# A hybrid decoder step: the state-space stage rebuilt in token layout, its projections split into three rounded products, and 16 dense steps placed beside the decode rows

## The reference, cut to what matters

```python
xbc, ssm_buf_new = causal_dwconv(xbc, ssm_buf, ssm_conv_w)
xbc = jax.nn.silu(xbc + ssm_conv_b).astype(f32)
xs_, Bm, Cm = split_cols(xbc, (SSM_DINNER, SSM_BC, SSM_BC))
dt = jax.nn.softplus(dt_raw.astype(f32) + ssm_dt_bias.astype(f32))
y_b, ssm_S_new = ssd_chunked(xs_, dt, A, Bm, Cm, ssm_S)      # per chunk:
#   y = (C B^T * decay) (x dt) + decay_in * (C S);  S = S * decay + B^T (decay_out * x dt)
y_b = (y_b + ssm_D[:, None] * xs_) * silu(z)
y_b = rmsnorm(y_b over each of 8 groups of 256 columns, ssm_norm_w)
```

## Time and profile before

| | |
|---|---|
| median of 3 runs | 3957.24 us (3954.14 to 3958.15) |
| profiled execution | 3952.51 us, span 3950.8 us |
| mean granted TensorE clock | 0.939 of full speed |
| TensorE matmuls busy | 3638.9 us (92%) |
| TensorE weight loads busy | 3120.4 us (79%) |
| VectorE | 1690.2 us (43%) |
| ScalarE | 843.3 us (21%) |
| GpSimd | 852.6 us (22%) |
| chain that ended last | TensorE 74%, VectorE 9%, issue 8%, ScalarE 3% |

### The profile page before, as it was taken

One profiled execution on the slowest core, in us unless ns is written; L12 is line 12 of the kernel. 1 busy time (PEld: TensorE's weight loads), 2 busy tenths in 40 slices (PEclk: granted clock), 3 DMA queues, 4 the chain that ended last, 5 costly groups with the idle time before them and its releaser, 6 DMA issues.

```text
span 3950.8 us, 53368 instructions
## 1 busy us (share of the span) xinstructions
PE 3638.9 (92%) x20671; PEld 3120.4 (79%) x20671; DVE 1690.2 (43%) x2840; ACT 843.3 (21%) x1709; POOL 852.6 (22%) x389
## 2 busy tenths in 40 slices
PE   6899999998899999999999977999988899999998
PEld 5888898887899766666666655667975799999998
DVE  4655556556300246566656671112024333323143
ACT  4333233333211122122212220001123111101010
POOL 3222323222122000000000000000322444444452
PEclk8999999998899999999999978999987899999999
DMA  3111011111222222212221225112422111111111
GB/s 113 45 44 39 28 32 38 43 38 33 71 81 70 63 65 77 79 52 59 76 81 49 76 88 198 59 43 64 134 69 85 32 53 44 43 48 48 47 44 64
DMA packets 317893, 248.31 MB, mean 63 GB/s; under 512 B 11028, under 2 KB 293213, under 8 KB 317717
## 3 DMA queue, kind: packets, MB, share of 16 engines
q1 hardware_dynamic: 282798, 211.28, 17.6%
q10 hardware_dynamic: 34992, 35.58, 2.6%
HBM read 200.50 MB, written 46.78 MB: 63 GB/s over the span
## 4 chain that ended last, share of the span: by engine, by line
PE 74%; DVE 9%; issue 8%; ACT 3%; POOL 2%; DMA 2%; ACTq 0%; DVEq 0%; SPq 0%; POOLq 0%
PE psum L894 22%; PE psum L1292 8%; PE psum L1294 8%; PE psum L1293 8%; PE psum L912 3%; PE psum L913 3%; PE psum L914 3%; PE psum L1028 2%; PE psum L1036 2%; PE psum L1040 2%; PE psum L868 2%; POOL wle L2687 1%; PE psum L1260 1%; PE psum L1323 1%; PE psum L1186 1%
## 5 line engine op out<-in xcount | busy, mean ns | idle before, releaser
L894 PE MATMUL psum<-xn,slab 128*128 128x344 f32 x2688 | 824.0, 464 | 29.4 <-ACT arena L1682 17.8
L894 PEld LDWEIGHTS psum<-xn,slab 128*128 128x128 f32 x2688 | 513.5, 194 | 304.3 <-issue 37.9
L2766 POOL TENSOR_SCALAR wparts<-slab 128x1024 fp32r<-128x1024 f32 x80 | 222.0, 2775 | 968.0 <-POOLq L68 968.0
L912 PE MATMUL psum<-xh,whe 128*128 128x344 f32 x1152 | 392.8, 341 | 16.3 <-POOL wle L2687 12.9
L913 PE MATMUL psum<-xl,whe 128*128 128x344 f32 x1152 | 373.2, 324 | 0.0
L914 PE MATMUL psum<-xh,wle 128*128 128x344 f32 x1152 | 372.4, 323 | 0.0
L1292 PE MATMUL psum<-at,wparts 128*128 128x344 f32 x960 | 308.8, 322 | 9.3 <-DVE r L2598 5.2
L1294 PE MATMUL psum<-at,wparts 128*128 128x344 f32 x960 | 307.6, 320 | 0.0
L1293 PE MATMUL psum<-xlow,wparts 128*128 128x344 f32 x960 | 306.9, 320 | 0.0
L2687 POOL TENSOR_TENSOR wle<-slab,whe 128x1024 fp32r<-128x1024 f32 x56 | 139.5, 2491 | 719.5 <-ACT whe L1433 719.5
L894 PE MATMUL psum<-arena,slab 128*128 128x344 f32 x768 | 229.1, 460 | 26.6 <-DMA arena<-d_yb 18.6
(11 more groups left out here) (385 smaller groups left out, 6319.7 us busy)
## 6 DMA issues: line engine op xcount, KB each, us to landing
slab<-in_w_in_dram SPq DMA_DIRECT2D x96, 512.0 KB, 4.0
arena<-d_rows SPq DMA_DIRECT2D x40, 512.0 KB, 5.1
slab<-in_w_ff_up_dram SPq DMA_DIRECT2D x32, 512.0 KB, 4.1
slab<-in_w_ff_down_dram SPq DMA_DIRECT2D x32, 512.0 KB, 3.9
out_dram<-arena ACTq DMA_DIRECT2D x24, 512.0 KB, 3.3
d_yb<-arena ACTq DMA_DIRECT2D x16, 516.0 KB, 5.9
...
```

The source lines that it names most:

```text
L894: mm = pe.matmul(psum[:, n, 0:GW], slabv[(base + u) % 2][:, k, :], src[:, k, n * GW:(n + 1) * GW], start=(k == 0 and u not in join), stop= ...
L912: pe.matmul(out, w_hi, a_hi, start=(k == 0), stop=False)
L2766: do(pool.tensor_scalar(rounded(wh[slot]), slab[slot][:, :], 1.0, None, ALU.mult))
```

## The change

- The projections of the state-space stage go through `project_parts`; slabs come in the order B, x, x, C, z, z; `high_weights` and `low_weights` are placed in ScalarE's and GpSimd's bodies; the sum of `xh` and `xl` is gone.
- The outputs are formed in token layout (`yt`): decay weights as stationary, x dt as moving operand; C times state is a product of its own, scaled on VectorE by `ecs`; z is transposed (tz) and multiplied in; the norm's sums come from ScalarE's squares with accumulation, the scale is applied on ScalarE, and 16 transposes (to0 to to3) turn y back.
- The decay differences move from VectorE to ScalarE (`decays`: eight relu with bias and one exp per tile). The broadcast decay rows come in four tiles of two chunks (`mlq`), the fourth over the first one once y1 is done.
- The skip term becomes a third product of the x transposes. The output tiles `yo` lie over `xdt` and `xdd`, so `wait(dve, yb_stored, 32 * g)` moves ahead of the x products.
- B and C of the sample rows are spread by products with a repeated column of the identity.
- `SFILL`: cb 24 becomes 8, decode 0 becomes 16.
- ScalarE's stores of the group before move behind the tb moves. In the last group SyncE issues the load of `ybv[0]` before the fourth decay tile.

Core of the diff:

```diff
+mlq = [carve(HPG * 2 * P) for _ in range(3)]
+mlq.append(mlq[0])
...
+yo = [arena[:, cut[0] - 4 * T + q * NT:cut[0] - 4 * T + (q + 1) * NT] for q in range(2)]
...
-SFILL = {"rw": 8, "tb": 8, "tx": 16, "cb": 24, "scan": 8, "fs": 8, "decode": 0, "norm": 16}
+SFILL = {"rw": 8, "tb": 8, "tx": 16, "cb": 8, "scan": 8, "fs": 8, "decode": 16, "norm": 16}
...
+    def csb_load(g, q):
+        last, group = ("y7", "y3", "y5", "y1")[q], g if q == 3 else g - 1
+        if not (isinstance(group, int) and group < 0):
+            sp.wait_ge(bank_full[ssm_plan.bank(last)], ssm_plan.after(last, group))
+            if not isinstance(group, int):
+                sp.sem_inc(sp_step, 1)
+        sp.dma_start(mlq[q].rearrange("p (r t) -> p r t", r=HPG),
+                     d_rows[bass.ds(HPG * g, HPG), q * 2 * P:(q + 1) * 2 * P].partition_broadcast(P)
+                     ).then_inc(csb_loaded[q % 3], 16)
...
+    def body(g, more, then):
         if more:
-            ssm_slab(g + 1, 0)
-            ssm_slab(g + 1, 1)
...
+            ssm_slab(g + 1, 3)
+        else:
+            upb_slab(0, 0, 0)
+            sp.wait_ge(yb_stored, 32 * SG_N // 2)
+            sp.wait_ge(proj_full, 3 * W_UPB)
+            sp.dma_start(ybv[0], d_yb[0:KT].rearrange("k p t -> p k t")).then_inc(yb_loaded[0], 16)
+        csb_load(g, 3)
+        if more:
+            ssm_slab(g + 1, 4)
+            csb_load(g + 1, 1)
+            csb_load(g + 1, 2)
+            ssm_slab(g + 1, 5)
+            csb_load(g + 1, 0)
+        if then:
+            ssm_slab(g + 2, 0)
+            ssm_slab(g + 2, 1)
...
+        project_parts(6 * g, W_SSM, m0, m1, lambda u, n: (proj_taken, 18 * g + (A_SSM + 3 * u + n - 2)),
+                      6 * [(xh, xl)])
...
+            def outputs(bk, c=c):
+                for r in range(HPG):
+                    head = slice(r * HD, (r + 1) * HD)
+                    yield pe.matmul(bk[:, head], cols(mlq[c // 2], 2 * r + c % 2),
+                                    xdt[:, 2 * P * c:2 * P * (c + 1)][:, head], start=True, stop=True)
                 if c:
...
+                    taken(G, f"su{c - 1}", g)
+                    yield pe.matmul(bk[:, 2 * P:4 * P], cols(cT, c), SST[c % 2], start=True, stop=True)
+
+            hand(G, f"y{c}", g, outputs)
+            if c == 1:
+                pe.wait_ge(z_ready, 2 * g + 2)
...
+                hand(G, f"tz{c // 2}", g, lambda bk, c=c: (
+                    pe.transpose(cols(bk, i), cols(zs[i % 2], c - 1 + i // 2), ident[:, :]) for i in range(4)))
             fill(f"scan{c}")
         taken(G, "su7", g)
...
+                hand(G, f"{name}{j}", g, lambda bk, j=j, part_=part_: (
+                    pe.matmul(cols(bk, i), ident[0:NB, 4 * j + i:4 * j + i + 1].broadcast_to([NB, P]),
+                              bc8[:, part_ * P:(part_ + 1) * P], start=True, stop=True) for i in range(4)))
...
+        pe.wait_ge(y8sq_ready, g + 1)
+        hand(G, "n8", g, lambda bk: (
+            pe.matmul(bk[:, 0:NB], ones[:, :], sq8[:, q * NB:(q + 1) * NB], start=(q == 0), stop=(q == 1))
+            for q in range(2)))
+        for p in range(4):
+            pe.wait_ge(ys_ready, NC * g + 2 * p + 2)
+            hand(G, f"to{p}", g, lambda bk, p=p: (
+                pe.transpose(cols(bk, i), yt[:, (2 * p + i % 2) * 2 * P + (i // 2) * P:][:, 0:P], ident[:, :])
+                for i in range(4)))
 
...
+    for u in range(6):
+        evacuate(0, 3 * u, 3 * u + 1)
+        high_weights((0, W_SSM + u + 1))
+        evacuate(0, 3 * u + 1, 3 * u + 3)
+        if 0 < u < 5:
+            stanh(0, u - 1)
...
+    def decays(g, q):
+
+        act.wait_ge(csb_loaded[q % 3], 16 * g + 16 if q in (1, 2) else 32 * g + 16 * (q // 3 + 1))
+        tile = mlq[q]
+        for i in range(2 * HPG):
+            r, c = i // 2, 2 * q + i % 2
+            ins = act.activation(cols(tile, i), cols(tile, i), ACT.Relu, scale=-1.0,
+                                 bias=shs[:, HPG * c + r:HPG * c + r + 1])
+        ins.then_inc(relu_ready, 1)
+        act.wait_ge(relu_ready, 4 * g + q + 1)
+        act.activation(tile, tile, ACT.Exp, scale=-1.0).then_inc(sdec_exp, 1)
...
-        for u in (4, 5):
...
         for j in range(2):
             move(G, f"tb{j}", g, half(btok, j), lambda bk: bk.rearrange("p (c i) -> p c i", c=4))
+        if not first:
+            stores(g - 1)
+        act.wait_ge(shs_ready, g + 1)
+        decays(g, 0)
         evac("tb")
...
+        if more:
+            high_weights((6 * g, W_SSM + 7))
+        act.activation(ecs, shs[:, 0:NC * HPG], ACT.Exp).then_inc(ecs_ready, 1)
+        decays(g, 1)
         evac("tx")
+        if more:
+            high_weights((6 * g, W_SSM + 8))
...
         evac("cb")
         for c in range(NC):
             evac(f"scan{c}")
             if more and c in (1, 3, 6):
-                stanh(g + 1, c // 2 if c < 6 else 2)
-        wait(act, stf_stored, 32 * g)
+                high_weights((6 * g, W_SSM + (9, 10, 11)[c // 2 - (c == 6)]))
+            if c == 2:
+                decays(g, 3)
+            if more and c in (2, 4, 6):
+                stanh(g + 1, c // 2 - 1)
+            if c >= 2:
+                squares(g, c - 2)
+        for c in range(NC - 2, NC):
+            squares(g, c)
...
+        act.wait_ge(srw_stored, 96 * g + 96)
         move(G, "fs", g, stf, lambda bk: bk[:, 0:2 * P])
...
         evac("decode")
...
+        act.wait_ge(ysq_ready, NC * g + NC)
+        act.activation(ssq, ssq, ACT.Sqrt, scale=1.0 / (2 * P), bias=eps[:, :]).then_inc(yroot_ready, 1)
+        move(G, "n8", g, r8[:, 0:NB], lambda bk: bk[:, 0:NB], ACT.Sqrt, scale=1.0 / (2 * P), bias=eps[:, :])
+        act.wait_ge(yrn_ready, g + 1)
+        for c in range(NC):
+            part_ = yt[:, 2 * P * c:2 * P * (c + 1)]
+            act.activation(part_, part_, ACT.Copy, scale=srn[:, c:c + 1]).then_inc(ys_ready, 1)
         evac("norm")
-
...
+        if then:
+            high_weights((6 * g, W_SSM + 12))
+        if more:
+            stanh(g + 1, 4)
+            stanh(g + 1, 5)
...
+        wait(dve, yb_stored, 32 * g)
         for j in range(4):
             bk = got(G, f"tx{j}", g).rearrange("p (c r e) -> p c r e", c=2, r=HPG)
-            for t, dst in ((dt, xdt), (dtd, xdd)):
+            for t, dst in ((dt, xdt), (dtd, xdd), (None, yt)):
                 ins = dve.tensor_tensor(
                     dst[:, 512 * j:512 * (j + 1)].rearrange("p (c r e) -> p c r e", c=2, r=HPG), bk,
+                    skip if t is None else
                     t[:, 2 * j:2 * j + 2, :].unsqueeze(3).broadcast_to([P, 2, HPG, HD]), ALU.mult)
             give(G, f"tx{j}", ins)
+        dve.wait_ge(shx_ready, g + 1)
...
+        def weights(q):
+
+            dve.wait_ge(sdec_exp, 4 * g + q + 1)
+            m = mlq[q].rearrange("p (r t) -> p r t", r=HPG)
+            dve.tensor_tensor(m, m, per_chunk(cbm[:, q * 2 * P:(q + 1) * 2 * P], HPG), ALU.mult
+                              ).then_inc(ml_ready, 1)
+
+        weights(0)
+        weights(1)
+        weights(2)
...
             give(G, f"su{c}", ins)
+            bk = got(G, f"y{c}", g)
+            y = yt[:, 2 * P * c:2 * P * (c + 1)]
+            if c:
+                dve.tensor_tensor(ytmp[c % 2].rearrange("p (r e) -> p r e", r=HPG),
+                                  bk[:, 2 * P:4 * P].rearrange("p (r e) -> p r e", r=HPG),
+                                  spread(ecs[:, HPG * c:HPG * (c + 1)], HD), ALU.mult)
+            ins = dve.tensor_tensor(y, y, bk[:, 0:2 * P], ALU.add)
+            give(G, f"y{c}", ins)
+            taken(G, f"y{c}", g)
+            if c:
+                do(dve.tensor_tensor(y, y, ytmp[c % 2], ALU.add))
             if c % 2:
-                name = f"y{c // 2}"
...
+                dve.wait_ge(z_ready, 2 * g + 2)
+                give(G, name, dve.tensor_tensor(pair, pair, bk, ALU.mult))
+                taken(G, name, g)
+                dve.sem_inc(yz_ready, 1)
+                if c == 3:
+                    weights(3)
             beside(f"scan{c}")
 
...
                                      stmp.rearrange("p (b n) -> p b n", b=4), AX_X, ALU.add))
+        do(dve.tensor_tensor(y8, y8, ysm, ALU.add))
+        do(dve.tensor_tensor(y8, y8, z8, ALU.mult))
+        dve.tensor_tensor(sq8, y8, y8, ALU.mult).then_inc(y8sq_ready, 1)
+        dve.wait_ge(yroot_ready, g + 1)
+        dve.reciprocal(srn, ssq).then_inc(yrn_ready, 1)
+        beside("end")
+        taken(G, "n8", g)
+        do(dve.reciprocal(r8[:, NB:2 * NB], r8[:, 0:NB]))
+        dve.wait_ge(ysq_ready, NC * g + NC)
...
+        for p in range(4):
+            bk = got(G, f"to{p}", g)
...
+    for index in range(7):
+        low_weights((0, W_SSM + index))
+
+    def body(g, more, then):
         lane.restart()
+        if more:
+            low_weights((6 * g, W_SSM + 7))
+        for index in range(8, 10):
+            if more:
+                low_weights((6 * g, W_SSM + index))
         pool.wait_ge(shx_ready, g + 1)
...
```

(3 more changed lines are left out.)

314 lines of the change are left out of this document (134 added, 180 removed).

## The result

| | before | after |
|---|---|---|
| median | 3957.4 us (3954.14 to 3958.15, 4 runs) | 3858.39 us (3847.06 to 3863.75, 4 runs) |
| profiled execution, span | 3952.51, 3950.8 us | 3863.75, 3862.0 us |
| granted TensorE clock, mean | 0.939 | 0.937 |
| TensorE busy | 3638.9 us (92%) | 3508.3 us (91%) |
| VectorE busy | 1690.2 us (43%) | 1731.5 us (45%) |

The ratio is 0.9748, 95% interval 0.9725 to 0.977: 99 us less by the medians. Medians and ratios in this document leave out two executions that ran slow as a whole, one of before (5304.7 us) and one of e10 (4064.5 us).

What follows compares the result with a forecast made beforehand. TensorE's own queue order was taken as the bound. Own steps -13.5, group 0 -23, groups 1 to 6 -85 and last group +13 gave -108 us, so 3849 us against the 3957.2 median; range 3815 to 3885, 60%.

Steps and rivals of the forecast that it cites:

- own steps: Group 0's own 18 dense chunks at the stage's start: 85.5 to 68.0 us, less some 4 for splitting; net -13.5.
- group 0: First group, waiting for no y store and with early weights: 104 us against 127.0, 23 less.
- groups 1 to 6: Middle groups of the state-space stage: 112 us each instead of 126.1, 85 us less in all.
- last group: Final group, where later state stores delay the next stage's y load: about 113 us against 100.2, 13 more.
- scans: From a group's first y product: TensorE 49.3 us, VectorE 50, nearly even; VectorE costs TensorE 0.5.
- Head of a group: From mark to first y product: 32.2 us, with 7.3 idle on weights and on VectorE held by the y store.
- head not late: Rival: stores issue in 2.0 and land at 15, no clock dip; group 105, time 3807 us; chance 17%.
- the clock's term: Slower TensorE clock after the stop before the first y product, priced at 2.5 us a group.
- GpSimd holds VectorE up: Rival: GpSimd's remainders stop VectorE, 8 us in each of 7 groups, 56 us, so 3905; chance 16%.
- Tail and clock: End of scans to root's product: 22.7 us, dense work covering VectorE's decode operations, granted clock 1.0.
- The 16 steps: Dense steps moved from beside the key products to the decode tail: the move costs 3 us a group.
- my chunk term: Each chunk of 8 dense steps falls from 4.63 to 3.78 us by split products, 15.3 us for a group's 18.

Runs made afterwards that it cites:

- e10: e9 with 8 of the 16 moved dense steps put back beside the key products; 3777.64 us.
- e4: Changed kernel with ScalarE issuing the previous group's stores first in its body, ahead of the rw copy and small stores; 3816.22 us.
- e3: Changed kernel with ScalarE rounding two weight slabs earlier, ahead of the root's copy and of the first decay tile; 3837.35 us.
- e5: Changed kernel with the four weight remainders that fall into a group's scans formed on VectorE instead of GpSimd; 3825.56 us.
- e6: Changed kernel with each of the four remainders in the scans followed on GpSimd by one more operation of its size; 3892.2 us.
- e1: Changed kernel with the 16 moved dense steps back beside the key products; 3860.81 us.
- e2: Changed kernel with whole float32 products in the stage's projections, without rounding and remainders, the rest of the rebuild kept; 3890.92 us.
- e9: Changed kernel with the edits of e3, e4 and e5 together; 3775.36 us.

## Why the prediction was right

The time came out inside the range, 92 us less at the end of the stage against a forecast of 108: own steps -12.7 (forecast -13.5), group 0 -22.4 (-23), groups 1 to 6 -64.4 (-85), last group +7.3 (+13). Inside a middle group the terms are less close than their sum:

| us | forecast | mean of groups 1 to 6 | group 3 |
|---|---|---|---|
| mark to first y product | 32.2 | 33.9 | 33.7 |
| scans | 49.8, and 2.5 for the clock | 51.2 | 49.7 |
| end of scans to root's product | 22.7 | 25.4 | 26.2 |
| root's product to next mark | 5.0 | 4.8 | 4.8 |
| group | 112.2 | 115.3 | 114.4 |

**Own dense steps: right.** The steps take 15.1 us less and start 2.4 later, -12.7 against -13.5. Copies of chunks stand 3.77 us apart (0.46 and 3.31 idle, at 1383.37 above), forecast 3.78. The split of the first slab shows in the start of the stage: 9.54 us idle, ended by GpSimd, where it was 6.07.

**Group 0: right.** 104.6 against 104. Its head waits neither for a y store nor for weights.

**Head of a group: right in kind, 1.7 us short, the stops not where I had them.** The y store held VectorE until 17.6 to 18.7 (forecast 17.2), as forecast. I had 7.3 us of stops: 2.1 and 1.2 for weights and, the largest, 4.0 ahead of the first y product. Five groups of six have 2.77, 2.0 to 2.2 and 2.1, which is about 7.0; group 3 has 2.17, 2.15 and none. The sum was right, but the third stop has another cause than the one I gave: in those five groups it is the 2.1 to 2.25 us for which GpSimd's third remainder held VectorE. Without that, an estimate from these rows, VectorE would have been ready at 31.6 to 31.9, when TensorE was. On ScalarE the six small stores issued faster than I took them (1745.34 to 1747.75, 2.4 instead of 3.95), the four large ones slower (3.75 instead of 1.9), and a decay tile took 3.5 instead of 2.7 (my own terms for it, 8 x 0.17 + 1.04, give 2.4). The rival "head not late" did not happen: e4 and e3 show that the stops of the head cost time. e4's 36 to 42 us lie near the 42 that I had put on that rival, but e4 also took away a weights stop and the meeting with GpSimd, so the agreement is in part luck.

**Scans: 1.1 us shorter than forecast with the clock's term, by other terms.** My 0.5 us for VectorE was 2.5 to 2.8 in five groups, a stop in scan 5, and it was the rival "GpSimd holds VectorE up" that made it. In group 2, where the remainder missed the carry, it was 1.6 in two stops. The clock behind the first y product was slow in the five groups with a stop there (0.66 to 0.83 over 10 us, as at 1889.20 above) and 1.00 in group 3. Against that I had the output products too high: 1.1 a chunk, of which the rows of the last group show 0.84 from start to start (L1210 at 2249.77, the product behind it at 2250.61).

**The rival "GpSimd holds VectorE up": it happened, in part.** It reaches TensorE in the head and in scan 5, and e5 took 27 to 33 us back, net of the 4.9 us of work a group that VectorE took over, where I had given 56. The other meetings, at 47 and 84 us behind the mark in group 3, stop TensorE nowhere in the rows. The row that I held against the rival, VectorE's eight additions at their usual pace, was weak evidence: the additions were already running when GpSimd's remainder began at 1311.52, and GpSimd was the one that waited. The Trainium skill (SBUF — State Buffer, "SBUF: two separate sides") says that whichever starts first keeps the ports for its whole instruction and the other waits. The rows of e6 agree with it in both directions, ends within 0.3 us of each other. The rows before the change hold one case that this does not cover: in the timeline of that kernel VectorE's last addition began at 1312.43, while GpSimd was already waiting, and still took its usual 1.23.

**Tail and clock: mis-sized.** From the end of the scans to the root's product I had 22.7 and it was 25.4 in the mean, 26.2 in group 3: there the decode rows took 4.36 instead of 3.6, and the four chunks behind them 17.7 instead of 15.1, because the granted clock fell to 0.66 right after those rows, with no stop in the 20 us ahead of it. I had forecast a clock of 1.0 there. It did not come in every group (group 2: rows 3.83, no fall, 111.0 us).

**Groups 1 to 6: the term that was mis-sized.** 115.3 against 112, so 64 us less instead of 85. It is made up of the tail (+2.7) and the head (+1.7), less 1.1 in the scans and 0.2 at the end: 3.1 on my 112.2.

**Last group: right in sign.** 107.5 against 113, 7.3 more than before instead of 13. The y load held the join until 30.1, not 34, after which the scans began at 46.7 instead of 51. The forecast's own terms (51 + 25 + 19 and the reload) add up to 111.7, not 113.

**The 16 steps: wrong in size.** I gave the move 3 us a group, 21 in all, against leaving the steps beside the key products. e1 shows 2 to 9 us, not told from nothing: the stops that I saw for the unmoved form came (a later y product, 1.8 instead of 0.9 us ahead of the root), but VectorE was further ahead in the later scans, and the stops of scan 5 and of the first y product went.

**Split against order.** By my chunk term the split should have brought 15.3 us to every middle group. e2 shows that it brought about nothing there (115.4 and 115.3) and its 33 to 38 us mostly in the own steps and group 0 (16.6 and 9.8). So in the middle groups the gain over the kernel before (126.1 to 115.3) is that of the new order alone (126.1 to 115.4). My sum came near it by setting 15.3 for the split against 9.8 of stops and slow clock; that the total came out is in part luck, and the expectation for e2, 3930 from terms of the same kind, missed by 39 us. The gain of the split went into two things that it brought itself: weights that TensorE must wait for in the head, and GpSimd's work against VectorE's. With the weights stops and most of GpSimd's share gone (it still forms two of a group's six remainders), and the stores early, a group takes 102.0 (e9), 13.4 less than the unsplit form, which is close to the 15.3. The unsplit form was not run with the stores early, so this is not shown; TensorE is busy 113.0 of its 116.0 us there, so there is little for that to win.

**Relu and exp.** I took no table load between them, and the rows show none.
